# Merge-gate projections moved into the prompt attention of a hybrid decoder step, with two PSUM banks taken from the attention

## The reference, cut to what matters

```python
h = _rmsnorm(x, lw['norm_mix_g'])
pr = _split_proj(jnp.einsum('btd,de->bte', h, lw['w_in']) + lw['b_in'])
...
u = jnp.einsum('btzc,zcd->btzd', jnp.stack([o_a, o_b, o_c], axis=2), w_branch)
g = jax.nn.sigmoid(gate_pre.reshape(B, T, N_BRANCH, D_MODEL))
return jnp.einsum('btd,de->bte', jnp.sum(g * u, axis=2), w_out)
```

## Time and profile before

| | us |
|---|---|
| median of three runs | 2447.22 |
| span of the profiled execution | 2447.7 |
| PE busy | 2199.6 (90%) |
| DVE busy | 852.1 (35%) |
| ACT busy | 666.5 (27%) |
| POOL busy | 328.9 (13%) |
| DMA, mean over the span | 52 GB/s |

### The profile page before, as it was taken

One profiled execution on the slowest core, in us unless ns is written; L12 is line 12 of the kernel. 1 busy time (PEld: TensorE's weight loads), 2 busy tenths in 40 slices (PEclk: granted clock), 3 DMA queues, 4 the chain that ended last, 5 costly groups with the idle time before them and its releaser, 6 DMA issues. The chain is left out here.

```text
span 2447.7 us, 38062 instructions
## 1 busy us (share of the span) xinstructions
PE 2199.6 (90%) x14280; PEld 1485.4 (61%) x14280; DVE 852.1 (35%) x1612; ACT 666.5 (27%) x1188; POOL 328.9 (13%) x245
## 2 busy tenths in 40 slices
PE   4889966799999884999699999987799999999998
PEld 2446633578778653666466666655466666666666
DVE  4211131667667536234322222223322222222223
ACT  5122221365465344332212221112211111111112
POOL 4200022300000001001100000000340330420410
PEclk7898978587698997999899999998899999999999
DMA  6421432000000302100321113021111111111111
GB/s 208 113 69 52 159 105 65 1 2 1 1 1 1 75 3 51 43 17 18 84 52 51 39 51 86 0 105 34 43 52 51 43 51 51 43 51 50 44 34 71
DMA packets 182794, 127.02 MB, mean 52 GB/s; under 512 B 8400, under 2 KB 175462, under 8 KB 182378
## 3 DMA queue, kind: packets, MB, share of 16 engines
q1 hardware_dynamic: 173258, 113.01, 15.8%
q0 software_dynamic: 4640, 10.60, 1.6%
q10 hardware_dynamic: 4800, 2.30, 0.3%
HBM read 111.68 MB, written 18.36 MB: 53 GB/s over the span
## 5 line engine op out<-in xcount | busy, mean ns | idle before, releaser
L426 PE MATMUL ps<-hH,wH 128*128 128x352 f16 x1536 | 318.3, 317 | 47.7 <-ACTq L399 27.8
L426 PE MATMUL ps<-hL,wH 128*128 128x352 f16 x1536 | 317.2, 316 | 0.0
L426 PE MATMUL ps<-hH,wL 128*128 128x352 f16 x1536 | 316.4, 315 | 0.0
L413 DVE SCALAR_TENSOR_TENSOR wL<-w,wH 128x1024 f16<-128x1024 f32 x98 | 120.1, 1225 | 322.0 <-ACT wH L406 307.7
L426 PEld LDWEIGHTS ps<-hH,wH 128*128 128x128 f16 x1536 | 151.3, 99 | 132.7 <-issue 48.3
L426 PE MATMUL ps<-mH,wH 128*128 128x352 f16 x960 | 196.2, 314 | 10.4 <-DVEq L399 8.1
L426 PEld LDWEIGHTS ps<-hL,wH 128*128 128x128 f16 x1536 | 151.9, 99 | 82.1
L426 PEld LDWEIGHTS ps<-hH,wL 128*128 128x128 f16 x1536 | 151.5, 99 | 81.2
L426 PE MATMUL ps<-mH,wL 128*128 128x352 f16 x960 | 196.0, 313 | 0.0
L426 PE MATMUL ps<-mL,wH 128*128 128x352 f16 x960 | 196.0, 313 | 0.0
L406 ACT ACTIVATE wH<-w 128x1024 f16<-128x1024 f32 x98 | 102.6, 1047 | 247.1 <-PE ps L426 225.4
(11 more groups left out here) (406 smaller groups left out, 2955.6 us busy)
## 6 DMA issues: line engine op xcount, KB each, us to landing
w<-in_mlp_w SPq DMA_DIRECT2D x64, 512.0 KB, 4.0
w<-in_w_in SPq DMA_DIRECT2D x32, 512.0 KB, 4.1
mgw<-in_w_in SPq DMA_DIRECT2D x24, 512.0 KB, 4.0
mgw<-in_w_branch SPq DMA_DIRECT2D x24, 256.0 KB, 4.3
xTd<-xT SPq DMA_DIRECT2D x1, 4224.0 KB, 12.3
xT<-xTd SPq DMA_DIRECT2D x1, 4224.0 KB, 14.0
xn<-in_x_prompt SPq DMA_DIRECT2D x8, 512.0 KB, 3.7
oH<-in_cache_nsa_cmp_kv SPq DMA_DIRECT2D x32, 128.0 KB, 3.0
```

Of the source, the lines that this page charges most:

```text
L413: self.k.nc.vector.scalar_tensor_tensor(self.k.wL[:, slot % 2, :, :], self.k.w32[:, slot, :, :], WS, self.k.wH[:, slot % 2, :, :], ALU.mul ...
L426: ins = nc.tensor.matmul(k.ps[:, 3 * parity + c, 0:CH], w[:, kt, :], x[:, kt, c * CH:(c + 1) * CH], start=(kt == 0 and x is inH and w is w ...
```

## The change

All 1728 gate matmuls leave `merge` and are issued inside `prompt_attention`. The PE does a run of 12 steps of three matmuls behind every fourth job (36 matmuls, one and a half column chunks of a gate tile), 12 runs per head, 48 in all. For them the attention gives up two PSUM banks: transposes now have bank 4 alone, outputs bank 5 alone, and banks 6 and 7 hold the gate sums. ScalarE gets the high part of 24 gate weight tiles and 72 copies of 352 columns with bias (no sigmoid yet) between its attention work, VectorE the 24 low parts. SyncE loads the weight tiles and stores each finished gate tile (128 x 1056, raw) to DRAM. ScalarE's hardware loop over the heads becomes straight code. `merge` keeps the 36 branch matmuls per unit, loads the raw gate from DRAM, applies the sigmoid in place, and now alternates its PSUM banks between units.

```diff
-            bank = (count[0] + count[1]) % 2
-            mine.append((bank, count[bank], count[0] + count[1], tiles[a:a + 4], a))
-            count[bank] += 1
+            mine.append((NG, tiles[a:a + 4], a))
+            NG += 1
...
-        C_SCORED, C_EXPED, C_TURNED, C_OUT, C_O, C_COMB = 2, 2, 5, 1, 3, 2
+        C_SCORED, C_EXPED, C_TURNED, C_OUT, C_O, C_COMB = 2, 2, 5, 1, 3, 1
...
+        T_BANK, O_BANK, D_BANK = 4, 5, 6
+        GT = 3 * KD // HPG
+        STEP = GT * 3 * KD // NJ
...
+        def gate_high(act, hh, n):
+            act.wait_ge(gate_in[n % 2], (hh * (GT // 2) + n // 2 + 1) * 16)
+            act.wait_ge(gate_mult, (hh * GT + n) * 3)
+            nc.scalar.activation(k.wH[:, n % 2, :, :], gw32[:, n % 2, :, :], ACT.Copy, scale=WS).then_inc(gate_hi, 1)
...
+        def gate_step(pe, hh, x):
+            n, c, kt = x // (3 * KD), x // KD % 3, x % KD
+            unit = 3 * n + c
+            if kt == 0:
+                if c == 0:
+                    pe.wait_ge(gate_lo, hh * GT + n + 1)
+                pe.wait_ge(gate_evac, hh * (3 * GT) + unit + 1)
+            for w, x in ((k.wH, k.hH), (k.wH, k.hL), (k.wL, k.hH)):
+                ins = nc.tensor.matmul(k.ps[:, D_BANK + unit % 2, 0:CH], w[:, n % 2, kt, :], x[:, kt, c * CH:(c + 1) * CH],
...
+        def gate_out(act, hh, n, c):
+            unit = 3 * n + c
+            act.wait_ge(gate_mult, hh * (3 * GT) + unit + 4)
+            if c == 0:
+                act.wait_ge(gate_stored, (hh * GT + n + 1) * 16)
...
+            nc.scalar.activation(gate_buf[:, n % 2, c * CH:(c + 1) * CH], k.ps[:, D_BANK + unit % 2, 0:CH], ACT.Identity,
+                                 bias=bias, scale=1 / WS).then_inc(gate_evac, 1)
...
-                    for bank, nth, _, tiles, a in groups[j]:
-                        pe.wait_ge(out[bank], hh * count[bank] + (nth - 1 + 1 + C_OUT))
+                    for order, tiles, a in groups[j]:
+                        pe.wait_ge(out, hh * NG + (order + C_OUT))
...
-                    pe.wait_ge(combined, hh * NJ + (j - 1 + C_COMB))
+                    pe.wait_ge(out, hh * NG + (groups[j][-1][0] + 1 + C_OUT))
+                    pe.wait_ge(combined, hh * NJ + (j + C_COMB))
...
                         if 2 <= j < NJ + 2:
                             turn(hh, j - 2)
+                            if j % 4 == 1:
+                                for x in range(at - 3 * STEP, at + STEP):
+                                    gate_step(pe, hh, x)
...
                     for j in range(NJ + 2):
+                        n, at = (j - 2) // 8, (j - 2) % 8
                         if j >= 2:
                             turned_out(act, nc.scalar.copy, hh, j - 2)
+                            if at == 0 and n:
+                                gate_out(act, hh, n - 1, 1)
+                            elif at == 1 and n:
+                                gate_out(act, hh, n - 1, 2)
+                            elif at == 2:
+                                gate_high(act, hh, n + 1)
+                            elif at == 4:
+                                gate_out(act, hh, n, 0)
...
+                        if 2 <= j < NJ + 2 and (j - 2) % 8 == 4:
+                            gate_low(dve, hh, (j - 2) // 8 + 1)
```

In `merge`:

```diff
-                sp.dma_start(w32[:, slot, 0:8, :], w_tile(d['w_in'], COL['merge'] + z * D + dt * P)).then_inc(loaded[slot], 16)
+                sp.dma_start(sg[:, u, :], k.gates[i]).then_inc(gate_in[u], 16)
...
+                    sp.wait_ge(branch_out, dt * 3 + u)
...
-                ins.then_inc(gate_mult, 1)
-                pe.wait_ge(branch_out, i + 2)
+                pe.wait_ge(branch_out, i + 1)
...
-                nc.scalar.activation(cols3(sg[:, u % 2, :]), dense_out(k.ps, 0), ACT.Sigmoid, bias=k.vec[:, bass.ds(b, 1)],
-                                     scale=1 / WS).then_inc(gate_out, 1)
+                act.wait_ge(gate_in[u % 3], dt * 16 + 16)
+                nc.scalar.activation(sg[:, u % 3, :], sg[:, u % 3, :], ACT.Sigmoid).then_inc(gated, 1)
```

More of the change, by code:

```diff
@@ L1058, in prompt_attention @@
     NJ = len(jobs)
-    groups, count = [], [0, 0]
+    groups, NG = [], 0
     for i, g, kind, tiles in jobs:
@@ L1110, in low, with _ @@
                 return eng.tensor_tensor(qP[half[1 - g], g * HPG + hh, :], k.qT[half[g], hh, 0:SEQ], qP[half[g], g * HPG + hh, :], ALU.subtract)
+            @block.sync
+            def _(sp):
+                sp.sem_inc(gate_stored, 32)
+                for n in range(2):
+                    sp.dma_start(gw32[:, n, :, :], w_tile(d['w_in'], gate_col(0, n))).then_inc(gate_in[n], 16)
+                for hh in range(HPG):
+                    for n in range(GT):
+                        sp.wait_ge(gate_lo, hh * GT + n + 1)
+                        sp.dma_start(gw32[:, n % 2, :, :], w_tile(d['w_in'], gate_col(hh, n + 2))).then_inc(gate_in[n % 2], 16)
+                        sp.wait_ge(gate_evac, hh * (3 * GT) + (3 * n + 5))
+                        sp.dma_start(k.gates[hh * GT + n],
+                                     gate_buf[:, n % 2, :]).then_inc(gate_stored, 16)
+                for n in range(2):
+                    sp.wait_ge(gate_in[n], 16 * (1 + HPG * GT // 2))
+                sp.wait_ge(gate_stored, 32 + 16 * HPG * GT)
             @block.gpsimd
@@ L1174, in _ @@
                             turn(hh, j - 2)
+                            if j % 4 == 1:
+                                for x in range(at - 3 * STEP, at + STEP):
+                                    gate_step(pe, hh, x)
             def turned_out(eng, copy, hh, j):
                 n = turned_rows(j)
-                for bank, nth, order, tiles, a in groups[j]:
+                for order, tiles, a in groups[j]:
                     eng.wait_ge(turned, hh * NG + (order + 1 + C_TURNED))
@@ L1183, in turned_out @@
                     copy(probT[0:n, j % 3, a:a + len(tiles), :].rearrange("p u n -> p (u n)"),
-                         k.ps[0:n, 4 + bank, 0:w]).then_inc(out[bank], 1)
+                         k.ps[0:n, T_BANK, 0:w]).then_inc(out, 1)
             @block.scalar
@@ L1189, in _ @@
                 act.sem_inc(exped, C_EXPED)
-                act.sem_inc(out[0], C_OUT)
-                act.sem_inc(out[1], C_OUT)
-                with act.Fori(0, HPG) as hh:
+                act.sem_inc(out, C_OUT)
+                act.sem_inc(gate_evac, 2)
+                act.wait_ge(gate_in[0], 16)
+                nc.scalar.activation(k.wH[:, 0, :, :], gw32[:, 0, :, :], ACT.Copy, scale=WS).then_inc(gate_hi, 1)
+                for hh in range(HPG):
                     for j in range(NJ + 2):
+                        n, at = (j - 2) // 8, (j - 2) % 8
                         if j >= 2:
                             turned_out(act, nc.scalar.copy, hh, j - 2)
+                            if at == 0 and n:
[6 more added lines that the diff above has]
+                                gate_out(act, hh, n, 0)
                         if j < NJ:
                             act.wait_ge(maxed, hh * NJ + (j + 1))
-                            before = groups[j - 3][-1][2] + 1 - (0 if j >= 3 else NG)
+                            before = groups[j - 3][-1][0] + 1 - (0 if j >= 3 else NG)
                             act.wait_ge(turned, hh * NG + (before + C_TURNED))
@@ L2007, in unit @@
                 pe.wait_ge(split_lo, i + 1)
-                pe.wait_ge(gate_out, i + 1)
-                for kt in range(KD):
-                    for w, x in ((wH, k.hH), (wH, k.hL), (wL, k.hH)):
-                        for c in range(3):
-                            ins = nc.tensor.matmul(k.ps[:, c, 0:CH], w[:, s, kt, :], x[:, kt, c * CH:(c + 1) * CH],
-                                                   start=(kt == 0 and w is wH and x is k.hH), stop=(kt == KD - 1 and w is wL))
-                ins.then_inc(gate_mult, 1)
-                pe.wait_ge(branch_out, i + 2)
+                pe.wait_ge(branch_out, i + 1)
                 for kt in range(4):
```

78 lines of the change are left out of this document (47 added, 31 removed).

## The result

The kernel after takes **2539.7 us** (median of 4 runs, 2535.6 to 2540.9) against 2449.6 us for the kernel before (4 runs, 2444.9 to 2458.3): a ratio of 1.0349 with an interval of 1.0316 to 1.0382. The direction was right; the size was not. The forecast was 2484 us and its range ended at 2530.

A forecast was written before the change was run, and what follows sets the result against it. The prediction took merge and late attention blocks as PE-bound, early blocks as slowed by a 0.50 clock and short jobs. Terms 0 + 63 + 13 - 8 - 48 + 7 + 2 + 7 = +36 us on 2447.7 gave 2484 us, range 2435 to 2530.

The forecast's parts named there:

- A: Moved gate matmuls: 258.7 us leave merge and 258.7 us arrive in the attention, by itself 0.
- rival 4: Attention: runs don't keep their rate between fp32 work, 0.165 us a matmul, 26 us more, 2510 us; chance 0.05.
- E: Early attention blocks (i of 0 to 3): runs cover waits, clock rises in a head's first run and stays: -48 us.
- B: Late attention blocks, one transpose bank: second groups wait 0.99 us for ScalarE's copy, 64 times: +63 us.
- C: Attention, one output bank: values wait for the previous job's combine, 0.41 us, 32 times in late blocks: +13 us.
- D: Late attention blocks: runs cover PE waits, 0.25 us back in each of 32: -8 us.
- F: Attention: gate work on ScalarE and VectorE; high parts can delay the first copy of a split group: +7 us.
- the start: Start of the attention: VectorE waits for a load and a split before its first maximum: +2 us.
- G: Merge: chain at every third unit 6, uncovered table loads 4, start gains -3: net +7 us.
- Rival 1: Attention: single banks cost nothing, replacing waits the PE has anyway: 2408 us; chance 0.10 in full, 0.17 for about half.
- Rival 2: Attention: the clock falls back between runs, early blocks gain only about -5: 2562 us; chance 0.08.
- Rival 3: Merge becomes bound by its chain of load, sigmoid, product: 2517 us; chance 0.10.

## Why the prediction was wrong, step by step

- **A** (0, and rival 4) held: gate matmuls start 0.149 to 0.150 us apart in the runs wherever the clock is up; where it is down (see E) they start 0.29 us apart.
- **B** (+63) was right in mechanism and nearly in size: 68 waits of 0.89 us, and +53 us alone (0.83 x 64).
- **C, late blocks** (+13) was twice as large when alone, 0.86 us a pair instead of 0.41, because the S values wait for the combine of C as the W values wait for that of S. Beside B's waits in the kernel after it added only 2.9 us a head (54.4 - 51.5), 11.4 in all: there the forecast is near by luck, one part left out and another covered. Together B and C cost the late blocks 15 us a head beside the runs (54.4 - 39.3), 60 in all; 66 was forecast between the marks.
- **D** (-8) was -1: runs cover nearly nothing in late blocks.
- **The late blocks as a whole** (+66 forecast, +74 measured) are near each other by luck: banks 60, D -1, and 14 us of falls of the clock, which the forecast did not have.
- **E is the step that failed**, -14.6 for -48: "At 1.5 runs per query block, with C: 5.9 + 6.6 + 7.1 + 9.4 = 29 us". The sum of PE work, VectorE's pace and the clock held to 6 us over the four heads with two banks of each kind (131.8 for 126). The words "with C" did not: 9.4 is 1.5 times 5.5 and two waits of 0.41, so C stands in it as the 0.41 us of a late block and for i = 3 only, about 5 us over the four heads, and B was taken to be absent; they cost 22 and 5 us. The mechanism is measured in the run with one output bank: after a run VectorE's queue is full, and the PE's wait is for what stands ahead of the combine, 1.02 us in the row shown, and the same in the kernel after. Nor did "I expect the clock to rise in the first run of a head and to stay": it fell back to 0.50 before the second run in all four heads of the kernel after, which is some 10 of the 27 us.
- **The steps between heads** grew by 14.7 us, of which the forecast holds the 7 that fall on the last pair of each head; it looked at jobs inside a head only. The issue gap of 2.81 us on VectorE stood in the trace of the kernel before.
- **F and the start** (+9): the start is +3.9 instead of +2; a copy of 352 columns took 0.55 us, not 0.46; what the copies and splits cost was not measured by itself, but neither the early blocks nor the late ones leave room for the +7.
- **G** (+10 for chain and table loads) was +12.3. Timeline of merge in the kernel after, at a third unit:

```profile
1653.24 2.19 POOL L2162 TENSOR_TENSOR mL<-mgacc,mH 128x1056 f32 x1 [15.48 <-ACT mH L2117]
...
1653.62 2.36 DVE L2131 SCALAR_TENSOR_TENSOR mgwL<-mgw,mgwH 128x512 f16<-128x512 f32 x1 [1.76 <-ACT mgwH L2106]
...
1656.04 0.62 PE L2096 MATMUL ps<-oH,mgwH 128*128 128x352 f16 x3 [1.39 <-DVE mgwL L2131]
...
1657.07 0.67 DVE L2131 SCALAR_TENSOR_TENSOR mgwL<-mgw,mgwH 128x512 f16<-128x512 f32 x1
```

The chain was the one forecast, but the split beside GpSimd's pass takes 2.36 us and not the 0.67 that it takes alone, and the PE waits 1.39 us for it. That happens at seven third units (waits from 1543 to 1692 us):

```profile
PE ps L2096 <- DVE mgwL L2131: 9.8, 7, 1.4
```

The PE has no other wait in that stretch, so the 4 us forecast for the table loads don't show; the remaining 2.5 us of the +12.3 are not traced.

- **Rival 1** (the banks cost nothing) is refuted by the three runs without a gate matmul. The Trainium skill's report of a kernel that gained nothing from double-buffered PSUM ("TensorE: Matmul & The Clock Gate", section "HAM oscillation — how this bites in real kernels") does not carry over: here a second bank is worth 76 us (transposes) and 61 us (outputs). **Rival 2** was right in part: 14 us in the late blocks and some 10 in the early ones, of the 78 that it would have cost, and the sign that the forecast gave against it (a clock of 1.00 from the first run on) did not show. **Rival 3** did not occur.

## What to carry to other kernels

When work is moved under a stage to fill its waits, look first at what it displaces there. Matmuls put in beside two banks of each kind gave 42 us, and the two PSUM banks that the moved ones took cost more than that. Price a lost buffer by the queue that stands ahead of its release on the other engine, at the moment when that queue is longest (here just after a run), and not by the length of the releasing instruction. Ask also whether the new waits leave the clock up. And look for room that is free in turns, like the second bank of a pair that narrow jobs leave empty, before taking room that is in use.

## What the runs showed of the hardware that was not expected

- A turn of a long loop on the PE and VectorE costs 3 to 6 us of issue gap in the place where it isn't covered (2.81 us on VectorE in the kernel before, 5.98 us on the PE in the kernel after), and is gone when the loop is written out.
- The same 321 PE instructions take 57 us at a clock of 0.97 and 82 at 0.58; with both banks single the clock was at its lower level in most of the late blocks of three heads of four, and the longest wait for another engine in these two stretches was 0.7 us at either clock.
- In the kernels with runs the clock rose in the first run of every head; with one output bank it fell to 0.50 again before the second run in three heads of four (with the transposes single too, in four), with two of each kind in one of four, and a fall cost about 3 us.
- A VectorE split of 128 x 512 took 2.36 us beside a GpSimd pass and 0.67 us alone.
